# A hybrid decoder step on one core: the sample tile's expert queries with rows stationary, the projection's prelude, the norm turn and the w_out product

## The chip, the cores and the metric

One Trainium2 chip, one core. The metric is device time of one launch in microseconds (us), as the median over runs. Engines: PE is TensorE (PEld its weight load), ACT ScalarE, DVE VectorE, POOL GpSimd, SP SyncE. All data are fp32.

## The reference, cut to what matters

```python
h = x + merged @ w_out
n2 = rms_norm(h, ln2_g)
y = h + peer(n2)                                  # 1024 prompt rows and 8*4 = 32 sample rows

def blk(xb):                                      # PEER: 8 heads, 128 keys per half, 16 experts per head
    qh = (xb @ wq).reshape(128, 8, 2, 128)
    s = einsum('thcd,hckd->thck', qh, keys)
    sv, si = top_k(s, 16)
    ...                                           # 16x16 candidates, top 16 of them: eidx, gates gw
    hpre = einsum('td,thkd->thk', xb, u_tab[eidx])
    act = gelu(hpre) * gw
    return einsum('thk,thkd->td', act, v_tab[eidx])
```

Ahead of it one projection of all rows is made: `rms_norm(x, ln1_g) @ w_in` (1024 x 11280), and `rms_norm(mem, mem_norm_g) @ w_mem_kv` for 256 memory rows. Attention and gated linear attention between the two stages are not touched.

## The kernel before, in words

**Projection (`project`).** Eleven tiles are normed and transposed first: eight of 128 prompt rows, one of 32 sample rows, two of memory rows. For each, SP loads the rows into one of two buffers `xin` (L166), ACT makes the root (square L268, logarithm L271, exponential L274), DVE scales the rows into `xn` (L313), PE transposes them in two halves (L335), ACT copies each half as the high part (L215) and DVE takes the low part (L222). ACT takes the root of tile t+1 before it copies tile t, DVE likewise. Then the first chunk of w_in (470 columns of 24 chunks) is split into high and low parts (ACT L228, DVE L233), and a loop of 12 pairs of chunks begins: PE makes three partial products for each of eight tiles (L344), and for the sample tile products on four column groups (`quarters`, L350: 32 stationary columns, 118 moving). Memory products come last. POOL loads w_in, and its first two chunks are asked for at the start. ACT's queue also moves caches and joins the two expert tables into `scratch_uv`.

**Experts (`experts`).** A turn is one head of one prompt tile (64 turns), or four heads of the 32 sample rows together (turns 64 and 65). Each turn has 16 rows k. POOL gathers row k's 128 table rows (8 KB each, L2233) into one of eight slots; DVE makes the dot product (L2437); ACT makes gelu, weight and a diagonal matrix (L2284, L2288, L2296); PE adds diagonal times row to the sum, two products of 512 columns (`sum_row`, L2571), which frees the slot. The order on every engine is written out by hand: PE runs `sum_row(turn, k)` for k = 0 to 15 and between them the queries of turn+3 (L2540, behind k = 4), its scores (L2553, behind k = 7), and for the next tile the transposed rows. Once per tile the next tile's `h` is made: merged rows are transposed (L2492, turn 1 of the tile, k = 8), the w_out product's 16 parts run behind odd k of turns 2 and 3 (L2503), DVE adds and squares in turn 4, ACT takes the root behind `exponents` of k = 8 in turn 4 (L2279, L2253, L2255), DVE norms the rows. Gelu and exponential lie in different tables of ACT, so each change between them is a load. The load of merged rows for the next tile is issued by SP after the previous tile's outputs are stored, which happens behind k = 3 of turn 0.

## Time and profile before

| | us |
|---|---|
| median of 3 runs | 4892.18 (4890.57 to 4895.22) |
| profiled execution | 4897.54 |
| its span | 4895.9 |
| mean granted clock of TensorE | 0.954 of full |

The profile's page gives busy time by engine, the chain of waits followed back from the last instruction, and groups of instructions by line. The trace behind it can be asked for any stretch. In the page TensorE is busy 86% of the span, VectorE 51%, ScalarE 36%, GpSimd 30%; DMA moves 335 GB/s on average. The projection fills the first 1153 us, the experts' stage the last 2800 us.

### The profile page before, as it was taken

Reading aid. Unit: us, or ns where it says so; the run is one execution under the profiler, and the core shown is the slowest. Engines: PE = TensorE matmul, PEld = TensorE weight load, DVE = VectorE, ACT = ScalarE, POOL = GpSimd, SP = SyncE. Lnnn points to the kernel's source line nnn. Section 1 sums busy time; section 2 is a strip of 40 time slices with the busy share of each in tenths; the row PEclk is TensorE's granted clock in tenths of the full one; section 3 lists DMA queues with packets and bytes.
Section 4 is the critical chain, followed back from the end, with each engine's and each line's share of the span. In section 5 each row is a group of like instructions: output and inputs, shape, how many; then the busy total and the mean of one; then the engine's idle time right before and its main releaser. Section 6 shows DMA issues by size and latency. Waiting matters only on the chain.

```text
span 4895.9 us, 55849 instructions
## 1 busy us (share of the span) xinstructions
PE 4225.6 (86%) x18768; PEld 2548.2 (52%) x18768; DVE 2516.4 (51%) x5454; ACT 1774.2 (36%) x4676; POOL 1491.4 (30%) x1435
## 2 busy tenths in 40 slices
PE   6999999996556788979889889898898888988997
PEld 5888888885434565434334344344343443433361
DVE  3111111115741673546666666666666666666645
ACT  3110111113511464324444444444444444444433
POOL 0000000003720551124444434344344444444433
PEclk9999999997668899989999999999999999999989
DMA  7799897882367783679999999999999999999979
GB/s 268 251 324 320 292 320 277 298 284 94 101 216 270 235 244 119 247 285 421 420 420 402 421 416 407 421 416 411 421 404 420 416 412 421 410 411 417 403 298 384
DMA packets 317396, 1642.02 MB, mean 335 GB/s; under 512 B 43832, under 2 KB 85656, under 8 KB 175224
## 3 DMA queue, kind: packets, MB, share of 16 engines
q0 software_dynamic: 164720, 1168.36, 58.3%
q1 hardware_dynamic: 116464, 248.64, 14.9%
q10 hardware_dynamic: 35984, 222.30, 13.6%
q8 instruction: 104, 1.70, 0.1%
q14 instruction: 124, 1.02, 0.1%
HBM read 1550.39 MB, written 318.03 MB: 382 GB/s over the span
## 4 chain that ended last, share of the span: by engine, by line
DMA 31%; PE 17%; ACT 4%; issue 3%; POOL 1%; DVE 0%; DVEq 0%; POOLq 0%; SPq 0%; ACTq 0%; PEldq 0%
DMA ex_rows<-scratch_uv,ex_E 31%; PE ex_ps_y L2571 13%; PE ex_ps_q L2540 3%; PE ex_ps_t L2503 1%; ACT ex_diag L2296 1%; POOL ex_rows L2233 1%; ACT ex_w L2288 1%; ACT ex_gel L2284 1%; ACT L2284 0%; ACT L2279 0%; ACT L2255 0%; ACT L2253 0%; PE ex_ps_s L2553 0%; PE ex_ps_y L2565 0%; DVE ex_dots L2437 0%
## 5 line engine op out<-in xcount | busy, mean ns | idle before, releaser
L2571 PE MATMUL ex_ps_y<-ex_rows,ex_diag 128*128 128x512 f32 (+1 forms) x4224 | 2016.0, 612 | 322.4 <-ACT ex_diag L2296 302.2
L2437 DVE CUSTOM_DVE_ANT_0 ex_rows<-ex_rows,ex_n2u 128x1024 f32<-128x1024 f32 x1056 | 1294.6, 1226 | 945.8 <-DMA ex_rows<-scratch_uv,ex_E 937.4
L2233 POOL DMA_INDIRECT ex_rows<-scratch_uv,ex_E x1056 | 1136.3, 1076 | 1681.4 <-PE ex_ps_y L2571 1547.9
L2571 PEld LDWEIGHTS ex_ps_y<-ex_rows,ex_diag 128*128 128x128 f32 (+1 forms) x4224 | 746.3, 189 | 1484.2 <-ACT ex_diag L2296 762.0
L344 PE MATMUL pj_ps<-pj_w_hi,pj_nT 128*128 128x470 f32 x3072 | 699.1, 378 | 23.0 <-PE pj_ps L350 13.1
L2284 ACT ACTIVATE ex_gel<-ex_dots 128x1 f32<-128x1 f32 x1056 | 214.0, 203 | 1361.9 <-DVE ex_dots L2437 1360.8
L344 PEld LDWEIGHTS pj_ps<-pj_w_hi,pj_nT 128*128 128x128 f32 x3072 | 580.2, 189 | 108.2 <-issue 28.8
L248 DVE COPY pj_zo<-pj_ps 128x470 f32<-128x470 f32 x96 | 61.4, 646 | 718.7 <-PE pj_ps L344 536.1
L2296 ACT ACTIVATE ex_diag<-ex_ident,ex_w 128x128 f32<-128x128 f32 x1024 | 411.1, 401 | 34.0 <-PE ex_ps_y L2571 0.5
L344 PE MATMUL pj_ps<-pj_w_lo,pj_nT 128*128 128x470 f32 x1536 | 362.3, 378 | 0.0
L248 ACT COPY pj_zo<-pj_ps 128x470 f32<-128x470 f32 x96 | 52.0, 553 | 826.3 <-PE pj_ps L344 484.3
L197 POOL DMA_DIRECT2D pj_w<-in_w_in x22 | 19.4, 883 | 1007.6 <-PE pj_ps L350 878.4
L2288 ACT ACTIVATE ex_w<-ex_gel,ex_gates 128x1 f32<-128x1 f32 x1056 | 311.1, 295 | 38.6 <-ACT ex_gel L2284 0.4
L344 PEld LDWEIGHTS pj_ps<-pj_w_lo,pj_nT 128*128 128x128 f32 x1536 | 291.9, 190 | 38.6
L2540 PEld LDWEIGHTS ex_ps_q<-ex_n2T,ex_wq 128*128 128x128 f32 x2304 | 287.1, 204 | 31.6 <-issue 30.1
L2540 PE MATMUL ex_ps_q<-ex_n2T,ex_wq 128*128 128x128 f32 (+1 forms) x2304 | 287.6, 286 | 1.1 <-ACT ex_n2T L2262 1.1
L233 DVE TENSOR_TENSOR pj_w_lo<-pj_w,pj_w_hi 128x3760 fp32r<-128x3760 f32 x28 | 114.1, 4074 | 159.9 <-ACT pj_w_hi L228 159.9
L2503 PE MATMUL ex_ps_t<-wo,ex_mT 128*128 128x512 f32 (+1 forms) x288 | 147.4, 603 | 1.1 <-ACT ex_mT L2244 1.1
L1516 PE MATMUL at_ps_b<-wb,at_ogT 128*128 128x512 f32 (+1 forms) x288 | 139.0, 604 | 9.4 <-DMA wb<-in_w_br_gla 7.4
L2096 PE MATMUL mg_ps_b<-wb,mg_aT 128*128 128x512 f32 (+1 forms) x288 | 129.0, 606 | 1.1 <-ACT mg_aT L2008 1.1
L1279 POOL TENSOR_TENSOR at_xr<-at_x,at_stat 128x1024 f32<-128x1024 f32 (+1 forms) x34 | 55.9, 1644 | 183.9 <-ACT at_stat L1315 82.8
L228 ACT CAST pj_w_hi<-pj_w 128x3760 fp32r<-128x3760 f32 x28 | 93.7, 3346 | 34.5 <-DMA pj_w<-in_w_in 23.1
(368 smaller groups left out, 3667.4 us busy)
## 6 DMA issues: line engine op xcount, KB each, us to landing
pj_w<-in_w_in POOLq DMA_DIRECT2D x24, 1880.0 KB, 18.0
scratch_z<-pj_zo SPq DMA_DIRECT2D x192, 235.0 KB, 10.9
scratch_uv<-in_peer_u ACTq DMA_DIRECT2D x8, 4096.0 KB, 25.4
scratch_uv<-in_peer_v ACTq DMA_DIRECT2D x8, 4096.0 KB, 43.0
scratch_uv<-in_peer_u ACTq DMA_DIRECT2D x4, 8192.0 KB, 41.6
scratch_uv<-in_peer_v ACTq DMA_DIRECT2D x4, 8192.0 KB, 72.1
out_dk_s<-in_cache_dil_k ACTq DMA_DIRECT2D x8, 4088.0 KB, 43.3
out_dv_s<-in_cache_dil_v ACTq DMA_DIRECT2D x8, 4088.0 KB, 55.2
```

The source lines that it names most:

```text
L233: nc.vector.tensor_tensor(w_lo[:, slot], w[:, slot], w_hi[:, slot], ALU.subtract).then_inc(w_lo_done, 1)
L344: last = nc.tensor.matmul(out, rows(a, k), weights(b, k), start=(m == 0 and k == 0), stop=(m == 2 and k == KD - 1))
L1516: last = nc.tensor.matmul(ps_b[0:width(t)], ogT[:, k, 0:width(t)], wb[:, k, 512 * half:512 * half + 512], start=(k == 0), stop=(k == KD - 1))
L2096: last = nc.tensor.matmul(ps_b[0:n, i % BANKS], aT[:, j, k, 0:n], wb[:, KD + k, 512 * c:512 * c + 512], start=(k == k0), stop=(k == k1 - 1))
L2233: pool.indirect_dma_start(out=rows[:, p % SLOTS, :], out_offset=None, in_=d["uv"], in_offset=bass.IndirectOffsetOnAxis(ap=E[:, turn % 4, k ...
L2284: nc.scalar.activation(gel[:, j, k:k + 1], dots[:, j, k:k + 1], ACT.Gelu).then_inc(gel_done, 1)
L2288: nc.scalar.mul(w[:, j, k:k + 1], gel[:, j, k:k + 1], gates[:, turn % 4, k:k + 1]).then_inc(w_done, 1)
L2296: nc.scalar.mul(diag[:, p % DIAGS, :], ident[:], w[:, j, k:k + 1]).then_inc(diag_done, 1)
L2437: nc.vector.tensor_tensor_reduce(out=row, in0=row, in1=n2u[:, tile % 2], scale=1.0, scalar=0.0, op0=ALU.mult, op1=ALU.add, accum_out=dots[ ...
L2503: last = nc.tensor.matmul(ps_t[0:n, 4 * c:4 * c + 4].rearrange("p k t -> p (k t)"), mT[:, k, 0:n], wo[:, k, 512 * c:512 * c + 512], start= ...
L2540: last = nc.tensor.matmul(ps_q[:, at:at + n], wq[:, k, head * 256 + c * P:head * 256 + (c + 1) * P], n2T[:, k, 0:n], start=(k == 0), stop= ...
L2571: last = nc.tensor.matmul(y[0:n, 512 * c:512 * c + 512], diag[:, p % DIAGS, 0:n], rows[:, p % SLOTS, D + 512 * c:D + 512 * c + 512], start ...
```

## The change

In `experts`: the two sample turns' queries are no longer 64 products with the weights stationary (128 columns) and 32 rows moving, but 32 products with the 32 rows stationary and 256 columns of weights moving, four heads at four groups of 32 output partitions, in two halves; ACT copies them to `qT`, PE transposes them, ACT copies again. An ordinary turn's queries are cut in two halves, behind k = 2 and k = 4. The w_out product's parts are spread over turns 0 to 3, the merged rows are transposed in turn 0 behind k = 7 (copied behind k = 9). In the norm turn one table set is loaded before the exponentials.

In `project`: three buffers of rows, asked for ahead of the constants; the weight loads wait for the second tile's landing; the first chunk is split behind tile 5; the two memory tiles are left out of the prelude, their roots are taken behind loop pass 7 and their transposes run between passes 8 and 9 and 9 and 10, so that each loop is cut into several.

```diff
@@ project
-        sq = zo[:].rearrange("p b c -> p (b c)")[:, 0:D]
+        spare = zo[:].rearrange("p b c -> p (b c)")
+        sq = spare[:, 0:D]
+        x_at = [xin[:, 0], xin[:, 1], spare[:, D:2 * D]]
+        HELD, SPLIT_AT = XT, 5
+        EARLY = 9
...
+            load_x(0)
             sp.dma_start(g1[:], d["ln1_g"].partition_broadcast(P)).then_inc(consts_in, 16)
+            load_x(1)
+            sp.dma_start(ident[:], d["ident"]).then_inc(consts_in, 16)
+            load_x(2)
             sp.dma_start(gm[:], d["mem_norm_g"].partition_broadcast(P)).then_inc(consts_in, 16)
-            sp.dma_start(ident[:], d["ident"]).then_inc(consts_in, 16)
...
             pool.sem_inc(w_used, 2)
+            pool.wait_ge(x_in[1], 16)
             for c in range(2):
                 pool.dma_start(w[:, c], w_dram[:, :, c * CW:(c + 1) * CW]).then_inc(w_in[c], 16)
...
-            take_hi(act, len(tiles) - 1)
-            split_hi(act, 0, 0, 0)
+            root(0)
+            for t in range(1, HELD):
+                root(t)
+                take_hi(act, t - 1)
+                if t == SPLIT_AT:
+                    split_hi(act, 0, 0, 0)
+            take_hi(act, HELD - 1)
...
+            root(HELD)
+            root(HELD + 1)
+            last_joins(DEC_B, EARLY)
+            take_hi(act, HELD)
+            last_joins(EARLY, EARLY + 1)
+            take_hi(act, HELD + 1)
+            last_joins(EARLY + 1, CHUNKS // 2)
...
+            chunk_pairs(0, EARLY)
+            turned(HELD)
+            chunk_pairs(EARLY, EARLY + 1)
+            turned(HELD + 1)
+            chunk_pairs(EARLY + 1, CHUNKS // 2)
@@ experts
+    OUT_AT = [(0, 14)] + [(turn, k) for turn in (1, 2, 3) for k in (0, 8, 10, 12, 14)]
...
+            def packed_queries(turn):
+                act.wait_ge(qs_done, turn - NT * PH + 1)
+                act.wait_ge(s_done, turn)
+                nc.scalar.copy(qT[:], ps_q[:, 0:2 * P]).then_inc(qs_out, 1)
...
+                        if k == 4 and packs(turn + 3):
+                            packed_queries(turn + 3)
...
+                    norms = k == 8 and turn % PH == 4 and turn < NT * PH
+                    if norms:
+                        nc.scalar.preload_act_table_set(TABLES)
                     if k == 8 and turn + 2 < TURNS:
                         exponents(turn + 2)
...
+            def packed_queries(turn, ks):
+                if 0 in ks:
+                    if opens(turn):
+                        pe.wait_ge(n2T_out, NT + 1)
+                    pe.wait_ge(qT_out, turn)
+                for k in ks:
+                    for i, head in enumerate(heads_of(turn)):
+                        last = nc.tensor.matmul(ps_q[i * NS:(i + 1) * NS, 0:2 * P], n2T[:, k, 0:NS], wq[:, k, head * 256:(head + 1) * 256],
+                                                start=(k == 0), stop=(k == KD - 1), skip_group_check=True)
+                if KD - 1 in ks:
+                    last.then_inc(qs_done, 1)
+            def turn_queries(turn):
+                pe.wait_ge(qs_out, turn - NT * PH + 1)
+                for c in range(2):
+                    last = nc.tensor.transpose(ps_q[:, (2 + c) * P:(3 + c) * P], qT[:, c * P:(c + 1) * P], ident[:])
+                last.then_inc(q_done, 1)
...
-                        if k == 4:
-                            queries(turn + 3)
+                        if packs(turn + 3):
+                            if k in (2, 3):
+                                packed_queries(turn + 3, range(4 * (k - 2), 4 * (k - 1)))
+                            if k == 5:
+                                turn_queries(turn + 3)
+                        elif k in (2, 4):
+                            queries(turn + 3, (k // 2 - 1,))
...
-                        if k == 8 and turn % PH == 1:
+                        if k == 7 and turn % PH == 0:
                             turn_merged(tile_of(turn) + 1)
-                        if k % 2 == 1 and turn % PH in (2, 3):
-                            out_product(tile_of(turn) + 1, (turn % PH - 2) * KD + k // 2)
+                        if (turn % PH, k) in OUT_AT:
+                            out_product(tile_of(turn) + 1, OUT_AT.index((turn % PH, k)))
```

PE's order in the turn that prepares turn 64, from the transposed sample rows (`ex_n2u`) to the scores. `ex_ps_y` is a row sum (two products each), `ex_ps_q` the queries; "x" is how many stand in a row. Before:

```order
L2524 MATMUL ex_ps_t<-ex_ident,ex_n2u 128x32 x8
L2571 MATMUL ex_ps_y<-ex_rows,ex_diag 128x512 x6
L2540 MATMUL ex_ps_q<-ex_n2T,ex_wq 128x32 x64
L2571 MATMUL ex_ps_y<-ex_rows,ex_diag 128x512 x6
L2553 MATMUL ex_ps_s<-ex_keysT,ex_qT 32x128 x8
```

The same place in the changed kernel:

```order
L2601 MATMUL ex_ps_t<-ex_ident,ex_n2u 128x32 x8
L2667 MATMUL ex_ps_y<-ex_rows,ex_diag 128x512 x2
L2628 MATMUL ex_ps_q<-ex_wq,ex_n2T 32x256 x16
L2667 MATMUL ex_ps_y<-ex_rows,ex_diag 128x512 x2
L2628 MATMUL ex_ps_q<-ex_wq,ex_n2T 32x256 x16
L2667 MATMUL ex_ps_y<-ex_rows,ex_diag 128x512 x4
L2637 MATMUL ex_ps_q<-ex_ident,ex_qT 128x128 x2
L2667 MATMUL ex_ps_y<-ex_rows,ex_diag 128x512 x4
L2649 MATMUL ex_ps_s<-ex_keysT,ex_qT 32x128 x8
```

64 products in one block have become two blocks of 16, with a row's sum between them, and two transposes.

ACT's order in the norm turn, behind row 8: `ex_ex` are the exponentials of turn+2, `ex_stat` the root. Before:

```order
L2279 ACT_TABLE_LOAD
L2279 ACTIVATE ex_ex,ex_esum<-ex_ex 128x16
L2253 ACT_TABLE_LOAD
L2253 ACTIVATE ex_stat<-ex_stat,ex_eps 128x1
L2255 ACT_TABLE_LOAD
L2255 ACTIVATE ex_stat<-ex_stat 128x1
L2284 ACT_TABLE_LOAD
L2284 ACTIVATE ex_gel<-ex_dots 128x1
```

The same place in the changed kernel:

```order
L2411 ACT_TABLE_LOAD
L2352 ACTIVATE ex_ex,ex_esum<-ex_ex 128x16
L2320 ACTIVATE ex_stat<-ex_stat,ex_eps 128x1
L2322 ACTIVATE ex_stat<-ex_stat 128x1
L2357 ACT_TABLE_LOAD
L2357 ACTIVATE ex_gel<-ex_dots 128x1
```

The two middle loads are gone.

PE's order in turn 3 of a tile, from behind row k = 1 to behind k = 7; `ex_ps_t` is a part of the w_out product. Before:

```order
L2503 MATMUL ex_ps_t<-wo,ex_mT 128x512
L2571 MATMUL ex_ps_y<-ex_rows,ex_diag 128x512 x4
L2503 MATMUL ex_ps_t<-wo,ex_mT 128x512
L2571 MATMUL ex_ps_y<-ex_rows,ex_diag 128x512 x2
L2540 MATMUL ex_ps_q<-ex_n2T,ex_wq 128x128 x16
L2571 MATMUL ex_ps_y<-ex_rows,ex_diag 128x512 x2
L2503 MATMUL ex_ps_t<-wo,ex_mT 128x512
L2571 MATMUL ex_ps_y<-ex_rows,ex_diag 128x512 x4
L2553 MATMUL ex_ps_s<-ex_keysT,ex_qT 128x128 x2
L2503 MATMUL ex_ps_t<-wo,ex_mT 128x512
```

Turns 1 to 3 in the changed kernel, from behind row k = 0 to behind k = 8:

```order
L2580 MATMUL ex_ps_t<-wo,ex_mT 128x512
L2667 MATMUL ex_ps_y<-ex_rows,ex_diag 128x512 x4
L2615 MATMUL ex_ps_q<-ex_n2T,ex_wq 128x128 x8
L2667 MATMUL ex_ps_y<-ex_rows,ex_diag 128x512 x4
L2615 MATMUL ex_ps_q<-ex_n2T,ex_wq 128x128 x8
L2667 MATMUL ex_ps_y<-ex_rows,ex_diag 128x512 x6
L2649 MATMUL ex_ps_s<-ex_keysT,ex_qT 128x128 x2
L2667 MATMUL ex_ps_y<-ex_rows,ex_diag 128x512 x2
L2580 MATMUL ex_ps_t<-wo,ex_mT 128x512
```

In rows 0 to 7 of turns 2 and 3 stood four parts and one query block of 16; now there is one part, in turns 1 to 3, and the block is in two.

## Rows read from the trace of the kernel before

**Rows 1.** The page, part 4: the chain that ended last, shares of the span.
```profile
DMA ex_rows<-scratch_uv,ex_E 31%; PE ex_ps_y L2571 13%; PE ex_ps_q L2540 3%; PE ex_ps_t L2503 1%; ACT ex_diag L2296 1%; POOL ex_rows L2233 1%; ACT ex_w L2288 1%; ACT ex_gel L2284 1%; ACT L2284 0%; ACT L2279 0%; ACT L2255 0%; ACT L2253 0%; P
```

**Rows 2.** Stretches: length, busy us of engines (instructions), TensorE clock, DMA share, GB/s.
```profile
2500.00:4636.00 2136.00, 1887.35 (x5556) 867.04 (x5555) 1423.12 (x3567) 960.35 (x2854) 897.79 (x833) 0.99 1.01 414
2672.00:2696.00 24.00, 21.77 (x52) 9.64 (x52) 16.77 (x42) 11.67 (x36) 13.07 (x10) 0.93 0.93 366
2696.00:2896.00 200.00, 169.38 (x502) 75.96 (x501) 130.60 (x329) 89.14 (x266) 77.65 (x78) 1.00 1.01 421
4536.00:4636.00 100.00, 98.72 (x292) 42.13 (x293) 68.27 (x173) 41.93 (x131) 45.64 (x39) 1.00 1.00 405
4640.00:4664.00 24.00, 19.07 (x45) 7.97 (x45) 15.15 (x37) 11.31 (x34) 10.18 (x10) 0.86 1.00 383
4672.00:4712.00 40.00, 40.00 (x168) 30.13 (x168) 15.11 (x33) 11.29 (x35) 7.84 (x9) 0.70 0.53 208
4728.00:4768.00 40.00, 40.00 (x174) 29.44 (x174) 15.77 (x34) 11.98 (x36) 8.36 (x10) 0.74 0.66 262
```

**Rows 3.** The chain in turn 18 (third tile): start, us, engine, tile, line.
```profile
2905.50 3.57 PE ex_ps_q L2540 x32
...
2910.79 0.86 PE ex_ps_t L2503 x2
2911.65 3.43 PE ex_ps_y L2571 x8
2915.08 0.44 PE ex_ps_s L2553 x4
```

**Rows 4.** The chain: the sample tile's two query blocks.
```profile
4670.82 23.66 PE ex_ps_q L2540 x128
...
4727.13 22.09 PE ex_ps_q L2540 x128
```

**Rows 5.** Timeline of TensorE, projection: start, us, shape, count [idle before].
```profile
104.73 1.82 PE L350 MATMUL pj_ps<-pj_w,pj_nS 128*32 128x118 f32 x64
...
106.97 1.97 PE L344 MATMUL pj_ps<-pj_w_hi,pj_nT 128*128 128x470 f32 x8 [0.42 <-PE pj_ps L350]
```

**Rows 6.** Timeline of ScalarE, norm turn of the third tile, first and last of four loads.
```profile
2995.59 1.28 ACT L2279 ACT_TABLE_LOAD   x1
...
3000.33 1.28 ACT L2284 ACT_TABLE_LOAD   x1
```

**Rows 7.** Timeline of TensorE: behind the norm turn's loads, and in an ordinary turn.
```profile
3002.64 18.77 PE L2571 MATMUL ex_ps_y<-ex_rows,ex_diag 128*128 128x512 f32 x36 [5.04 <-ACT ex_diag L2296]
...
3080.00 2.41 PE L2571 MATMUL ex_ps_y<-ex_rows,ex_diag 128*128 128x512 f32 x5 [0.96 <-ACT ex_diag L2296]
```

**Rows 8.** Timeline of the projection's start, all engines.
```profile
2.67 31.04 SPq L166 DMA_DIRECT2D pj_xin<-in_x_prompt  x8
...
16.49 1.05 ACT L215 CAST pj_nT<-pj_ps 128x512 fp32r<-128x512 f32 x2
...
26.09 0.59 ACT L215 CAST pj_nT<-pj_ps 128x512 fp32r<-128x512 f32 x1 [0.62 <-PE pj_ps L335]
...
39.20 0.59 ACT L215 CAST pj_nT<-pj_ps 128x512 fp32r<-128x512 f32 x1 [0.62 <-PE pj_ps L335]
...
46.32 0.48 DVE L222 TENSOR_TENSOR pj_nT<-pj_ps,pj_nT 128x128 fp32r<-128x128 f32 x2
...
46.75 1.94 PE L335 MATMUL pj_ps<-pj_ident,pj_xn 128*128 128x128 f32 x8 [1.32 <-DVE pj_nT L222]
...
53.13 3.33 ACT L228 CAST pj_w_hi<-pj_w 128x3760 fp32r<-128x3760 f32 x1
...
56.49 4.07 DVE L233 TENSOR_TENSOR pj_w_lo<-pj_w,pj_w_hi 128x3760 fp32r<-128x3760 f32 x1 [2.53 <-ACT pj_w_hi L228]
...
60.70 3.50 PE L344 MATMUL pj_ps<-pj_w_hi,pj_nT 128*128 128x470 f32 x8 [8.09 <-DVE pj_w_lo L233]
```

**Rows 9.** The experts' loads of merged rows: from issue to landing.
```profile
DMA to landing us min/median/max: 9.1/11.6/20.6
```

More of the change, by code:

```diff
@@ L307, in _, with normed @@
             dve.wait_ge(consts_in, 48)
-            for t, (row, n, mem) in enumerate(tiles):
+            def normed(t):
+                row, n, mem = tiles[t]
                 dve.wait_ge(rms_done, t + 1)
@@ L328, in _, with turned @@
             pe.wait_ge(consts_in, 48)
-            for t, (row, n, mem) in enumerate(tiles):
+            def turned(t):
+                row, n, mem = tiles[t]
                 pe.wait_ge(xn_done, t + 1)
@@ L338, in _ @@
                     last.then_inc(halves_done, 1)
-            pe.wait_ge(lo_out, 2 * len(tiles))
+            for t in range(HELD):
+                turned(t)
+            pe.wait_ge(lo_out, 2 * HELD)
             def product(out, rows, weights):
@@ L2178, in heads_of, with packs @@
             return [turn % PH] if turn < NT * PH else [(turn - NT * PH) * PACK + i for i in range(PACK)]
+        def packs(turn):
+            return turn >= NT * PH
         def width(tile):
@@ L2267, in queries @@
                     act.wait_ge(s_done, turn)
[L2268 removed]
+                nc.scalar.copy(qT[:], ps_q[:, 2 * P:] if packs(turn) else ps_q[:, 0:2 * P]).then_inc(qT_out, 1)
+            def packed_queries(turn):
+                act.wait_ge(qs_done, turn - NT * PH + 1)
+                act.wait_ge(s_done, turn)
+                nc.scalar.copy(qT[:], ps_q[:, 0:2 * P]).then_inc(qs_out, 1)
             def scores(turn):
@@ L2525, in turn_rows, with queries @@
                 last.then_inc(n2_t, 1)
-            def queries(turn):
-                tile, heads = tile_of(turn), heads_of(turn)
-                n = width(tile)
-                if opens(turn):
-                    pe.wait_ge(n2T_out, tile + 1)
-                if turn == 1:
-                    pe.wait_ge(wq_in, 16)
-                if turn:
-                    pe.wait_ge(qT_out, turn)
-                for i, head in enumerate(heads):
-                    for c in range(2):
-                        at = (2 * i + c) * n
-                        for k in range(KD):
-                            last = nc.tensor.matmul(ps_q[:, at:at + n], wq[:, k, head * 256 + c * P:head * 256 + (c + 1) * P], n2T[:, k, 0:n],
-                                                    start=(k == 0), stop=(k == KD - 1))
+            def queries(turn, halves=(0, 1)):
+                tile, (head,) = tile_of(turn), heads_of(turn)
+                if 0 in halves:
+                    if opens(turn):
+                        pe.wait_ge(n2T_out, tile + 1)
+                    if turn == 1:
+                        pe.wait_ge(wq_in, 16)
+                    if turn:
+                        pe.wait_ge(qT_out, turn)
+                for c in halves:
+                    for k in range(KD):
+                        last = nc.tensor.matmul(ps_q[:, c * P:(c + 1) * P], wq[:, k, head * 256 + c * P:head * 256 + (c + 1) * P], n2T[:, k],
+                                                start=(k == 0), stop=(k == KD - 1))
+                if 1 in halves:
+                    last.then_inc(q_done, 1)
```

105 lines of the change are left out of this document (63 added, 42 removed).

## The prediction

> **What bounds the kernel now.** Read the chain of waits first [rows 1]. It reaches back only to the start of the experts' stage (2096 us, the last 2800 us of the span), and two thirds of it there is gathers landing and the row sums behind them. So the first question is how full the DMA engines are, and the table of stretches answers it [rows 2]. In a quiet stretch (2696 to 2896) the engines move 421 GB/s, share 1.01: nothing but fewer bytes would help there. A gather is 128 rows of 8 KB, 1.05 MB, so 2.49 us at that rate, and a turn of 16 gathers cannot take under 39.8 us. Time is lost only where the rate falls below 421. I turn each rate into lost time as length x (421 - rate)/421, and ask which edit removes that loss.
>
> The losses fall in three places [rows 2]. (a) The two turns that prepare the sample tile's queries: 4672 to 4712 at 208 GB/s loses 20.2 us, 4728 to 4768 at 262 loses 15.1 us; 35.3 us together. (b) A 24 us stretch after the norm turn of each tile, at 366 in 2672 and 383 in 4640: 3.1 and 2.2 us. (c) The 100 us before it, in which the w_out product is interleaved; in the last tile they run at 405, 3.8 us lost. The row 2500 to 4636 holds the rest of (b) and (c): 414 over 2136 us loses 35.5 us for six norm turns and seven product stretches, and the norm turn at 4640 adds 2.2, so 37.7 us. I give (b) 7 x 2.9 = 20 us and the rest, 17 us, to (c), 2.4 us per tile.
>
> Why a stall of TensorE becomes lost DMA time: a gather needs one of eight row slots, and a slot is free only when TensorE has summed its row. TensorE needs 1.72 us per row (3.43 us for two) against 2.49 us per gather [rows 3], so it catches up 0.77 us per row, 12 us per turn.
>
> The stage before, the projection, is a different case: there TensorE issues products back to back from 60.70 us on, so whatever delays the first product delays everything [rows 8].
>
> **The change, part by part.**
>
> *Packed queries.* Before, each of the two turns issues 64 products of 32 columns against a full 128x128 weight load: 23.66 and 22.09 us during which no row is summed [rows 4]. TensorE's clock there reads 0.70 and 0.74 of full as a mean, so much of it runs at 1.2 GHz instead of 2.4 [rows 2]. Afterwards there are 32 products of 256 columns, the rows stationary (32 columns), four heads on four column groups, in two halves behind rows 2 and 3, then a copy and two transposes behind row 5. The trace has this very shape: the projection's sample quarters, 32 products of 118 columns on four groups, took 1.82 us [rows 5]. Scaled by 256/118 that is 3.9 us per turn. Streamed without any overlap between groups, at half of the 512-column product's 0.86 us [rows 3], it would be 32 x 0.43 = 13.7 us. I take 3.9, since only the row of the quarters has the four groups. That is the size of an ordinary turn's query block, 3.57 us [rows 3], which costs no DMA time in the quiet stretch, and it now comes in halves of 2 us. The additions: two transposes of about 0.24 us each (8 took 1.94 us) [rows 8], a second copy, and TensorE's wait for that copy behind row 5. ScalarE makes it after diagonal 4, before TensorE gets to row 5, so two row sums (3.4 us) hide it; behind ScalarE's own wait for the products stands the weight of row 5, due a gather later. I charge 1.3 us for both turns. **Gain 34 us**, ends 24 (no overlap: 27.4 us of products instead of 45.8, the excess over the catch-up lost) and 35.3.
>
> Around the quarters TensorE is idle for 0.42 us before the next full-width product [rows 5]; eight such edges in the two turns come to 3.4 us spread over 80 us, below the catch-up. The Trainium skill ("TensorEngine Tiling (Array Packing)", Key Properties) says that changing the tiling mode drains TensorE, which speaks against splitting the queries into halves; the trace agrees that there is a gap, and puts 0.42 us on it. The term stays 34 us by either.
>
> *Norm turn.* ScalarE loads four tables in a row, 1.28 us each, from 2995.59 to 3001.61 [rows 6]; TensorE waits 5.04 us and then needs 18.77 us for nine rows, 2.09 each instead of 1.72, at a lower clock [rows 2, 7]. An ordinary turn has two loads and a wait of 0.96 us [rows 7], and its stretch shows no loss. With the set that holds both logarithm and exponential loaded ahead, the two middle loads go: 2 x 1.28 = 2.57 us off ScalarE in each of eight tiles, and what remains is an ordinary turn plus 0.5 us. Tile 0's norm turn lost almost nothing, so seven count. **Gain 18 us** of 20; ends 8 (only the 2.57 us of ScalarE count, and TensorE arrives late from (c) anyway) and 20.
>
> The Trainium skill ("ScalarE: Activation LUTs", What ACT_TABLE_LOAD costs) gives a switch about 2.66 us, half of it a drain ahead of the load. Here four loads of 1.28 us and the activations between them fill 6.02 us in all, with no room for drains, so the measurement decides; by the page the edit would take 5.3 us off each norm turn instead of 2.57, which could not return more than the 20 us lost.
>
> *w_out and the split of ordinary queries.* Eight products of 0.86 us per turn behind odd rows of turns 2 and 3 become one in turn 0 and five in each of turns 1 to 3; the query block of 3.57 us is cut in two, behind rows 2 and 4. TensorE's load in turns 2 and 3 was 16 x 1.72 + 3.57 + 0.44 + 8 x 0.86 = 38.4 of 39.8 us; now 35.8 in turns 1 to 3. Between rows 0 and 7 it was 7.4 us of extras against 8 x 0.77 = 6.2 of catch-up; now 4.9. That turns a deficit into a surplus. **Gain 11 us** of 17; ends 2 (the total of products is the same, and turn 1 now has them as well) and 17. The merged rows are transposed behind row 7 of turn 0 rather than row 8 of turn 1. They are requested right after the previous tile's outputs (row 3) and land 11.6 us later [rows 9]; four rows at 2.49 us plus 1.5 MB of other traffic at 421 (3.6 us) make 13.5 us, so the wait is about nothing. Queued behind it on TensorE would be the row sums.
>
> *Prelude.* The first product waits for the whole chain of eleven tiles, then for the first weight chunk's split, 3.33 on ScalarE and 4.07 on VectorE [rows 8]. The sample tile's low parts were done at 46.80. Now (1) the tiles' rows are asked for first and the weights after the second tile has landed. From the first tile's copy at 16.49 to the third's at 26.09 pass 9.6 us, where two steady steps are 6.6 (26.09 to 39.20 are four steps, 3.28 each): 3.0 us, and the first request moves up from 2.67 to the place of the first constant, 1.8 us, together 4.8; (2) the split sits in the chain after tile 5 and adds 3.33 on ScalarE and about 2.4 where VectorE's 4.07 holds up the next norm. First product at 46.8 - 4.8 + 5.7 = 47.7 instead of 60.70: 13.0 us. Against it, the two memory tiles are transposed on TensorE inside the projection, 2 x 1.94 us in full, and the loop is cut in three. No row shows such a cut; from one product group to the next TensorE idles 0.42 us [rows 5], so I add 1 us and keep 3 for the low end. Their roots and norms lie beside products on the other engines. **Gain 8 us**, ends 4 and 11.
>
> **Sum.** 34 + 18 + 11 + 8 = 71 us. The profiled execution spans 4895.9 us, 4897.54 with what lies around it, 5.4 above the median of 4892.18. Losses of 71 us from it and from the median are the same work, so I predict 4892 - 71 = **4821 us**. All terms at their low ends give 38 (4854), all at their high ends 83 (4809).
>
> **Rivals.**
> *No overlap of the column groups*: halves of 6.9 us; the term falls to 24, so 4831. For: matmuls of one shape run in order. Against: the quarters' 1.82 us. 8 in 100.
> *The norm and w_out losses move instead of going*: rates stay near 365 and 412 because the slots, not the bursts, limit them, and turn 1 joins in. Gain 34 + 8 + 8, so 4842. For: the amount of products is unchanged. Against: the quiet stretches at 421 with the same slots. 13 in 100.
> *The prelude gives nothing*: the tables' and caches' transfers now start when the products do, and the first banks wait for their stores: 4829. 7 in 100.
> *Slower*: the merged rows come late. If their load took 20.6 us, the longest one [rows 9], rather than 11.6, TensorE would stand 9 us behind row 7 in each of eight tiles, 72 us, plus the 3 us of low clock that the norm turn's 5 us wait shows, 24 us: 71 - 96 = 25 us slower, 4917. It decides from about 5.5 us of extra landing time per tile. Against: seven loads of this place have the median 11.6, the longest is from the stage's start. 2 in 100.
> Main case 70 in 100.
>
> **Chances.** A measurement of this kernel can tell about 0.2% (10 us) from no change. All cases but the last are faster by more: 0.96, within 0.02, slower 0.02. The range of 8 in 10 runs from 4806 (all high ends and 3 us more) to 4846 (the second rival with a smaller prelude).
>
> **What would show it.** Right: query groups of the sample turns with 64 entries of 32x256 taking about 4 us, no stretch near 4700 below 400 GB/s; two table loads in a norm turn, its stretch near 420; 100 us before it near 418; first product near 48 us and no gap of TensorE at loops above 2 us. Wrong: products of 0.4 us one after another; a wait of TensorE for the h rows in turn 0; the lost rate found again at rows 8 to 15 of turns 0 and 1.

## The result

| | us | |
|---|---|---|
| before | 4893.1 | 4890.57 to 4895.22, 4 runs |
| changed | **4851.53** | 4850.49 to 4852.78, 4 runs |
| ratio | 0.9909 | 95% interval 0.9897 to 0.9922 |
| forecast | 4821 | range 4806 to 4846 |

The change is faster by 41.6 us, where 71 were forecast. The direction was right; the size was wrong, and the time lies 5.5 us outside the range. The profiled execution took 4852.27 us with a span of 4850.6, against 4895.9 before.

Put beside [rows 2], the table of stretches after (columns as there: length, busy us of PE, PEld, DVE, ACT and POOL with their instructions, TensorE's granted clock, DMA share, GB/s). In order: the quiet part of the stage, the second tile's norm turn with its two loads, 200 us of an ordinary stretch, the last tile's product stretch, its norm turn, and the two turns with the packed queries.

```profile
2500.00:4620.00 2120.00, 1893.40 (x5534) 870.65 (x5533) 1418.52 (x3555) 933.41 (x2828) 971.76 (x830) 0.99 1.01 416
2656.00:2680.00 24.00, 19.28 (x44) 7.24 (x42) 16.67 (x38) 12.06 (x37) 11.78 (x10) 1.00 1.01 411
2696.00:2896.00 200.00, 174.58 (x501) 79.64 (x501) 130.18 (x330) 87.56 (x263) 90.02 (x78) 0.98 1.01 418
4520.00:4620.00 100.00, 94.92 (x283) 41.57 (x284) 69.88 (x179) 41.95 (x131) 46.94 (x40) 1.00 1.00 413
4624.00:4648.00 24.00, 17.23 (x34) 6.83 (x35) 15.07 (x34) 8.92 (x29) 12.40 (x9) 0.93 1.01 392
4656.00:4696.00 40.00, 35.14 (x158) 13.72 (x154) 27.09 (x72) 17.93 (x55) 18.34 (x17) 1.00 1.01 415
4700.00:4740.00 40.00, 32.65 (x84) 11.58 (x83) 26.91 (x68) 17.98 (x55) 18.20 (x17) 1.00 1.01 421
```

The packed turns are as forecast: 415 and 421 GB/s instead of 208 and 262, at the full clock of 2.4 GHz. The norm turns rose only part of the way to the 420 of the forecast: 411 instead of 366 GB/s in the second tile, 392 instead of 383 in the last. The product stretch has 413 instead of 405, where 418 was forecast. And the row over the whole quiet part says 416 instead of 414, where the two terms for it (18 and 11 us) asked for 419.

TensorE in the first packed turn, timeline (start, us, line, shape, count, idle before in brackets):

```profile
4654.53 1.02 PE L2667 MATMUL ex_ps_y<-ex_rows,ex_diag 128*128 128x512 f32 x2
4655.48 1.93 PE L2628 MATMUL ex_ps_q<-ex_wq,ex_n2T 128*32 128x256 f32 x32
4657.35 3.70 PE L2667 MATMUL ex_ps_y<-ex_rows,ex_diag 128*128 128x512 f32 x8
4660.88 0.38 PE L2637 MATMUL ex_ps_q<-ex_ident,ex_qT 128*128 128x128 f32 x2
4661.10 3.60 PE L2667 MATMUL ex_ps_y<-ex_rows,ex_diag 128*128 128x512 f32 x8
```

A half takes 1.93 us (1.95 were forecast from [rows 5]), the transposes 0.38, and TensorE waits for nothing between. The gap of 0.42 us at a change of shape [rows 5], which the Trainium skill's "TensorEngine Tiling (Array Packing)" (Key Properties) leads one to fear for eight edges, does not stand here: between full-width row sums and column groups no idle time is listed. (In the projection such a gap is still there: 0.55 us at 843.10 below.)

ScalarE's loads and TensorE's wait in the second tile's norm turn, against [rows 6, 7]:

```profile
2657.98 1.28 ACT L2411 ACT_TABLE_LOAD   x1
...
2660.02 1.28 ACT L2357 ACT_TABLE_LOAD   x1
...
2662.33 5.42 PE L2667 MATMUL ex_ps_y<-ex_rows,ex_diag 128*128 128x512 f32 x12 [2.33 <-ACT ex_diag L2369]
```

The same turn of the kernel before:

```profile
2673.74 17.41 PE L2571 MATMUL ex_ps_y<-ex_rows,ex_diag 128*128 128x512 f32 x36 [4.08 <-ACT ex_diag L2296]
```

Two loads instead of four, and a wait of 2.33 us instead of 4.08. The projection, against [rows 8]:

```profile
47.35 3.10 PE L397 MATMUL pj_ps<-pj_w_hi,pj_nT 128*128 128x470 f32 x7 [1.14 <-DVE pj_nT L234]
...
843.10 1.07 PE L385 MATMUL pj_ps<-pj_ident,pj_xn 128*128 128x128 f32 x8 [0.55 <-PE pj_ps L403]
```

The first product starts at 47.35 (47.7 forecast, 60.70 before), and a memory tile's eight transposes inside the loop take 1.07 us, not 1.94.

So the loads, the waits and the products came out as forecast, the rates rose at least part of the way, and 30 us are missing. The page's chain has the gathers at 36% of the span (31% before, [rows 1]) and the row sums at 9% (13%): the stage was bound by landings before and is bound by them now.

```profile
DMA ex_rows<-scratch_uv,ex_E 36%; PE ex_ps_y L2667 9%; PE ex_ps_q L2615 1%; ACT ex_diag L2369 1%; ACT ex_w L2361 1%; PE ex_ps_t L2580 1%; ACT ex_gel L2357 1%; ACT L2357 0%; ACT L2352 0%; PE ex_ps_y L2661 0%; DVE ex_dots L2514 0%; DVE ex_rows L2514 0%; POOL ex_rows L2300 0%; ACT ex_mT L2311 0%; ACT ex_ex L2352 0%
```

### The profile page after: what moved, and what is told of

Read it like the earlier page. It is cut to its first block, busy times and chain, and to the rows that moved or that the text cites. A ratio compares the mean times of both kernels' runs of the same rounds, so it can differ in the third digit from the quotient of the medians.

```text
span 4850.6 us, 55532 instructions
## 1 busy us (share of the span) xinstructions
PE 4210.5 (87%) x18644; PEld 2516.7 (52%) x18644; DVE 2514.9 (52%) x5454; ACT 1748.6 (36%) x4662; POOL 1586.1 (33%) x1435
## 4 chain that ended last, share of the span: by engine, by line
DMA 36%; PE 12%; issue 4%; ACT 4%; DVE 1%; POOL 0%; DVEq 0%; POOLq 0%; ACTq 0%; SPq 0%; PEldq 0%
DMA ex_rows<-scratch_uv,ex_E 36%; PE ex_ps_y L2667 9%; PE ex_ps_q L2615 1%; ACT ex_diag L2369 1%; ACT ex_w L2361 1%; PE ex_ps_t L2580 1%; ACT ex_gel L2357 1%; ACT L2357 0%; ACT L2352 0%; PE ex_ps_y L2661 0%; DVE ex_dots L2514 0%; DVE ex_rows L2514 0%; POOL ex_rows L2300 0%; ACT ex_mT L2311 0%; ACT ex_ex L2352 0%
## 5 line engine op out<-in xcount | busy, mean ns | idle before, releaser
L2300 POOL DMA_INDIRECT ex_rows<-scratch_uv,ex_E x1056 | 1231.8, 1167 | 1548.0 <-PE ex_ps_y L2667 1401.8
L2615 PEld LDWEIGHTS ex_ps_q<-ex_n2T,ex_wq 128*128 128x128 f32 x2048 | 250.6, 193 | 59.9 <-issue 56.7
L2615 PE MATMUL ex_ps_q<-ex_n2T,ex_wq 128*128 128x128 f32 x2048 | 251.5, 277 | 1.1 <-ACT ex_n2T L2329 1.1
```

The costliest lines, as they stand in the source:

```text
L2300: pool.indirect_dma_start(out=rows[:, p % SLOTS, :], out_offset=None, in_=d["uv"], in_offset=bass.IndirectOffsetOnAxis(ap=E[:, turn % 4, k ...
L2615: last = nc.tensor.matmul(ps_q[:, c * P:(c + 1) * P], wq[:, k, head * 256 + c * P:head * 256 + (c + 1) * P], n2T[:, k], start=(k == 0), st ...
```

## Where the missing time was: nowhere

The forecast turned each rate below 421 GB/s into lost time. The trace of the kernel before had the means to test that. VectorE makes a row's dot product the moment the row has landed, so its starts are the landings. Here they are through the third tile's norm turn, the very place at which ScalarE loads four tables (2995.59 to 3001.61), TensorE waits 5.04 us [rows 6, 7] and the rate dips to 373 GB/s; rows in between are left out:

```profile
2996.00:3020.00 24.00, 18.96 (x38) 7.91 (x37) 17.32 (x40) 14.16 (x38) 10.92 (x9) 0.86 0.93 373
```

```profile
2998.31 1.23 DVE L2437 CUSTOM_DVE_ANT_0 ex_rows<-ex_rows,ex_n2u 128x1024 f32<-128x1024 f32 x1 [1.16 <-DMA ex_rows<-scratch_uv,ex_E]
...
3000.79 1.22 DVE L2437 CUSTOM_DVE_ANT_0 ex_rows<-ex_rows,ex_n2u 128x1024 f32<-128x1024 f32 x1 [0.64 <-DMA ex_rows<-scratch_uv,ex_E]
...
3005.76 1.23 DVE L2437 CUSTOM_DVE_ANT_0 ex_rows<-ex_rows,ex_n2u 128x1024 f32<-128x1024 f32 x1 [0.19 <-DMA ex_rows<-scratch_uv,ex_E]
...
3008.24 1.23 DVE L2437 CUSTOM_DVE_ANT_0 ex_rows<-ex_rows,ex_n2u 128x1024 f32<-128x1024 f32 x1 [1.16 <-DMA ex_rows<-scratch_uv,ex_E]
...
3023.15 1.23 DVE L2437 CUSTOM_DVE_ANT_0 ex_rows<-ex_rows,ex_n2u 128x1024 f32<-128x1024 f32 x1 [0.40 <-DMA ex_rows<-scratch_uv,ex_E]
```

From 2998.31 to 3023.15 stand ten steps in 24.84 us: 2.484 each, the full pace, through the stall. (Between 3000.79 and 3005.76 one dot product started late, behind VectorE's own norm; the next stands at its place again.) In the second tile's norm turn, the one of [rows 2] with 366 GB/s, a single landing is 0.32 us late. Nothing was lost there, so nothing could be won.

That gives a theory. **Theory A:** landings go on at 2.485 us as long as a stall of TensorE is shorter than what the eight row slots hold in flight; only what goes beyond is lost. **Rival B:** the forecast's reading, each us of a lower rate is lost. Both explain the packed turns (stalls of 22 to 24 us); they part on everything short.

To compare kernels better than by medians, which differ by some us from chip to chip for the same kernel, I use two lengths of each trace: from the start of the second tile's first gather to that of the last prompt tile's (768 gathers), and from there to the end. The start of a gather is its issue, and a stall just ahead of it can move that without moving a landing; where this matters I count from the landing instead, that is from VectorE's first dot product of the second tile.

| kernel | six tiles | to the end | sum |
|---|---|---|---|
| before | 1969.7 | 462.7 | 2432.5 |
| changed | 1965.0 | 431.3 | 2396.3 |
| changed, another chip | 1967.2 | 431.2 | 2398.5 |

The two traces of the changed kernel differ by 2.2 us, and the spread is wider than that: the kernel before with the new prelude alone (below), whose experts' stage is unchanged, has a sum of 2427.7, 4.8 us less than the kernel before. The six tiles gave 3 to 5 us, which is within this spread; the last tile and the sample turns gave 31.4.

## Experiment 1: each part alone

**Packed queries alone**, in the kernel before:

```diff
-                        if k == 4:
+                        if packs(turn + 3):
+                            if k in (2, 3):
+                                packed_queries(turn + 3, range(4 * (k - 2), 4 * (k - 1)))
+                            if k == 5:
+                                turn_queries(turn + 3)
+                        elif k == 4:
                             queries(turn + 3)
```

> The kernel before with the sample tile's packed queries alone. Theory A (gathers land at the DMA's own pace, 2.49 us each, and only a stall longer than the row slots cover delays a landing): the landings of turns 61 and 62 were late by 14.6 and 13.0 us plus some 3.7 us around them in the trace of before; 29 to 32 us faster. Rival B (every microsecond at a rate below 421 GB/s is lost time): 34 to 35 us faster.

Measured: 4865.96 us (4864.88 to 4869.3), ratio 0.9942 [0.9928, 0.9955], 28.4 us less than before. That is below the range of either theory, and the interval (22 to 35 us) holds both. The sum of the table is 2397.8, which is 34.6 us below the kernel before and 29.9 below the unchanged stage of the next run. So this run cannot tell A from B. It shows where the gain is: with 2396.3 and 2398.5 for the changed kernel, the whole of its gain behind the projection is in this part.

**Prelude alone** (`project` of the changed kernel, the rest of the kernel before):

```diff
+            load_x(0)
             sp.dma_start(g1[:], d["ln1_g"].partition_broadcast(P)).then_inc(consts_in, 16)
+            load_x(1)
...
+            chunk_pairs(0, EARLY)
+            turned(HELD)
+            chunk_pairs(EARLY, EARLY + 1)
+            turned(HELD + 1)
```

> The kernel before with the projection's new prelude alone. The projection ended 10.5 us earlier in the changed kernel's trace, but the experts began only 7.5 us earlier. Theory A and B alike: 8 to 10.5 us faster if the stages between are neutral; 5 to 7.5 if the 3 us lost between them belong to the change.

Measured: 4880.37 us (4878.78 to 4882.47), ratio 0.9971 [0.996, 0.9981], 14.0 us less, more than either expected. The projection's last product ended at 1138.7 instead of 1152.9, 14.2 us earlier. The products' loop gives back next to nothing of the 13.4 us by which the first product moved up: the sample tile's product groups start 13.7 us earlier in the first pass and in the last (91.0 against 104.7, 1101.2 against 1114.9), since the two passes that carry transposes are 0.6 us longer and the others about 0.1 us shorter. Between the projection and the experts stands a stage that no edit touches. It takes 990.6 to 998.2 us from trace to trace, so what the prelude is worth is read from the projection and from the medians, not from where one trace's experts begin. In the changed kernel's own first trace the last product ended at 1142.3: one pass lost 2.8 us there, in which TensorE waits 2.09 us for VectorE's split of a weight chunk, and its second trace (1139.1) has nothing of it.

**Table load ahead of the norm turn's exponentials, alone:**

```diff
+                    norms = k == 8 and turn % PH == 4 and turn < NT * PH
+                    if norms:
+                        nc.scalar.preload_act_table_set(TABLES)
                     if k == 8 and turn + 2 < TURNS:
                         exponents(turn + 2)
```

> The kernel before with one table set loaded ahead in the norm turn (16 of 32 loads fewer over eight tiles). Theory A: the dots went on at 2.49 us through the stall, so 0 to 3 us faster. Rival B: the dips to 366 GB/s are lost time, 16 to 20 us faster.

Measured: 4899.93 us (4891.98 to 4904.48, 11 runs), ratio 1.001 [1.0001, 1.0019], so 5.6 us more, with an interval that just excludes zero; sum of the table 2432.7 against 2432.5. A had 0 to 3 us less. The traces show no change in the stage, and what makes the median higher is open. There is no gain where the forecast had 18 us. B falls.

**The w_out product spread, merged rows earlier, ordinary queries in halves, alone:**

```diff
-                        if k == 8 and turn % PH == 1:
+                        if k == 7 and turn % PH == 0:
                             turn_merged(tile_of(turn) + 1)
-                        if k % 2 == 1 and turn % PH in (2, 3):
-                            out_product(tile_of(turn) + 1, (turn % PH - 2) * KD + k // 2)
+                        if (turn % PH, k) in OUT_AT:
+                            out_product(tile_of(turn) + 1, OUT_AT.index((turn % PH, k)))
```

> The kernel before with the w_out product spread over turns 0 to 3, merged rows transposed in turn 0 and ordinary queries in halves; nothing else. Theory A: landings of turns 2 and 3 were late by 0.5 to 1 us per tile, so 2 to 6 us faster. Rival B: 11 to 17 us faster.

Measured: 4891.95 us (4887.59 to 4898.06, 11 runs), ratio 0.9993 [0.9984, 1.0002], 2.4 us less. Its sum in the table is 2423.9, which is 8.6 us less than before but only 3.8 less than the unchanged stage in the prelude's run; one trace of each, so I leave it at somewhere between 0 and 9 us.

**Packed queries and prelude together, without the other two:** the same question from the other side.

> The kernel before with the packed sample queries and the new prelude alone, without the table load ahead of the norm turn's exponentials and without the spread of the w_out product, the earlier merged rows and the halves of ordinary queries. Theory A (landings go on through stalls shorter than the slots' cover): those parts are worth 0 to 5 us, so 4851 to 4857. Rival B (my forecast's reading, 18 and 11 us for them): 4875 to 4885.

Measured: 4848.15 us (4846.49 to 4851.82), ratio 0.9908 [0.9891, 0.9924]; sum of the table 2397.6. Against the kernel before on the same chip it is 45.4 us less, more than A's 36 to 42 and far from B. That is the changed kernel (ratio 0.9909 [0.9897, 0.9922], sums 2396.3 and 2398.5). Once the packed queries are in, the norm turn's edit and the w_out edit cannot be seen at all.

## Experiment 2: how long a stall the slots cover

A direct test of A: put stalls of known length where there were none. Into the changed kernel, with n = 1, 3 or 5:

```diff
+                    if k == 12 and turn % PH >= 5 and turn < NT * PH - 3:
+                        for i in range(n):
+                            nc.scalar.activation(stall[:, 2 * i:2 * i + 1], eps[:], ACT.Exp).then_inc(stalled, 1)
+                            nc.scalar.activation(stall[:, 2 * i + 1:2 * i + 2], eps[:], ACT.Gelu).then_inc(stalled, 1)
```

Each exponential and each gelu needs its own table set, so each pair costs ScalarE two loads, 3.03 us in all (loads of two neighbouring pairs start 3.03 us apart in the trace).

> The changed kernel with one pair of table loads more (a small exponential and a small gelu on a scratch column) on ScalarE behind row 12 of turns 5, 6 and 7 of each of the first seven tiles: 21 places, about 3.0 us each (two loads of 1.28 us and two small activations). TensorE then waits some 2.5 us for a diagonal. Theory A (a stall costs only what is beyond the cover of the eight row slots, 7 to 8 us): within 3 us of the changed kernel, 4849 to 4855. Rival B (every us of a lower rate is lost, my forecast's reading, by which a wait of 5 us costs 2.9): 1.5 us each, 31 more, 4875 to 4895.

> The same with three pairs in a row, about 9.0 us on ScalarE at the 21 places; TensorE waits about 8.5 us. Theory A: 0 to 1.5 us beyond the cover at each place, so 0 to 32 more, best guess 4870. Rival B: at least 5 us each, 105 more or over, 4955 to 4990.

> The same with five pairs in a row, about 15 us on ScalarE; TensorE waits about 14.5 us. Theory A: 14.5 less 7 to 8 of cover is 7 us each, 150 more (130 to 175), 4980 to 5025; from three pairs to five the whole 6 us of each place is paid, 126 us. Rival B: 8.7 us or more each, at least 183 more, 5035 or over, and it rises in proportion from one pair to five.

| pairs | TensorE waits | median (range) | ratio to before | sum of the table | from the second tile's first landing to the end |
|---|---|---|---|---|---|
| 0 | | 4851.53 | 0.9909 [0.9897, 0.9922] | 2396.3 | 2381.4 (2383.5 on another chip) |
| 1 | 1.1 to 1.9 us | 4847.89 (4845.0 to 4848.48) | 0.9899 [0.9883, 0.9916] | 2396.3 | 2381.4 |
| 3 | 6.6 to 8.0 us | 4853.31 (4852.39 to 4853.87) | 0.9912 [0.9896, 0.9929] | 2396.3 | 2385.4 |
| 5 | 12.5 to 14.0 us | 4979.12 (4976.4 to 4986.28) | 1.0174 [1.0157, 1.0191] | 2508.8 | 2498.4 |

The cost has a knee. Three pairs cost next to nothing: 2 to 4 us of landings for the 18 stalls behind the second tile's first landing, and a median 5.4 us above that of one pair on the same chip, for 21 stalls; at most 0.3 us each, for waits of 7.4 us on average. (The sum of the table hides this, since a stall of the first tile delays the issue at which it begins by 4 us.) From three pairs to five the median rises 125.8 us for 21 stalls, 6.0 each, and ScalarE's two pairs more are 6.06 us: from there on every us is paid. Against one pair, five cost 6.2 us each of a mean wait of 13.2, so some 7 us are covered. A's range held for three pairs, though its best guess of 4870 was too high, and it missed for five by 0.9 us (4980 to 5025), since the waits were 1.3 us shorter than expected. B's straight line (at least 105 us for three pairs) is gone.

Three pairs, TensorE's wait, then VectorE's starts and the rate of the 24 us around it:

```profile
3410.34 9.86 PE L2676 MATMUL ex_ps_y<-ex_rows,ex_diag 128*128 128x512 f32 x18 [7.09 <-ACT ex_diag L2371]
```

```profile
3403.10 1.22 DVE L2523 CUSTOM_DVE_ANT_0 ex_rows<-ex_rows,ex_n2u 128x1024 f32<-128x1024 f32 x1 [1.17 <-DMA ex_rows<-scratch_uv,ex_E]
3405.59 1.22 DVE L2523 CUSTOM_DVE_ANT_0 ex_rows<-ex_rows,ex_n2u 128x1024 f32<-128x1024 f32 x1 [1.18 <-DMA ex_rows<-scratch_uv,ex_E]
3408.39 1.22 DVE L2523 CUSTOM_DVE_ANT_0 ex_rows<-ex_rows,ex_n2u 128x1024 f32<-128x1024 f32 x1 [1.42 <-DMA ex_rows<-scratch_uv,ex_E]
3410.83 1.22 DVE L2523 CUSTOM_DVE_ANT_0 ex_rows<-ex_rows,ex_n2u 128x1024 f32<-128x1024 f32 x1 [0.81 <-DMA ex_rows<-scratch_uv,ex_E]
```

```profile
3396.00:3420.00 24.00, 16.91 (x35) 7.14 (x34) 16.61 (x44) 17.05 (x42) 10.13 (x9) 0.86 1.00 406
```

The same for five pairs:

```profile
3429.31 12.21 PE L2676 MATMUL ex_ps_y<-ex_rows,ex_diag 128*128 128x512 f32 x24 [13.17 <-ACT ex_diag L2371]
```

```profile
3430.89 1.23 DVE L2523 CUSTOM_DVE_ANT_0 ex_rows<-ex_rows,ex_n2u 128x1024 f32<-128x1024 f32 x1 [0.38 <-DMA ex_rows<-scratch_uv,ex_E]
3438.64 1.23 DVE L2523 CUSTOM_DVE_ANT_0 ex_rows<-ex_rows,ex_n2u 128x1024 f32<-128x1024 f32 x1 [6.09 <-DMA ex_rows<-scratch_uv,ex_E]
3442.09 1.23 DVE L2523 CUSTOM_DVE_ANT_0 ex_rows<-ex_rows,ex_n2u 128x1024 f32<-128x1024 f32 x1 [1.43 <-DMA ex_rows<-scratch_uv,ex_E]
```

```profile
3416.00:3440.00 24.00, 10.83 (x22) 4.74 (x22) 13.35 (x39) 18.57 (x43) 5.46 (x5) 0.72 0.69 278
```

Three pairs: a wait of 7.09 us, and the landings come 2.49, 2.80 and 2.44 us apart. TensorE's row sums of 1.7 us against 2.49 us per landing let it catch up behind the stall before the next one. Five pairs: 13.17 us, and the step from 3430.89 to 3438.64 is 7.75 us, 5.3 late, the next one 3.45, another 1.0 late. The slots ran dry, as A has it; that it is the eight slots which set the 7 us is argued, for no run has another number of them. The DMA share comes nearer to telling them apart than the rate: 1.00 with three pairs, 0.69 with five, and 0.53 and 0.66 in the two sample query blocks of the kernel before, but 1.00 in the norm turn at 4640 and the product stretch at 4536 [rows 2], from which the forecast took its 2.2 and 3.8 us of loss. It is no measure either: at 2672 it was 0.93, with 0.32 us of delay.

## Experiment 3: what the rest of a tile's time is

128 gathers at 2.485 us are 318.1 us, a tile takes 327.5. In every tile landings are late at two kinds of places. Four gathers in turn 0 (k = 6 to 9) are 0.2 to 1.3 us late, together about 4 us, where outputs are stored and the next h and x rows come in. The others stand alone: a landing 0.97 us late every 21 to 25 gathers, five or six per tile, at the same rows in kernels whose TensorE, ScalarE or GpSimd work differs. With the projection of the kernel before, in which VectorE's program is another, the same pattern stands at other rows. In the changed kernel I count 39 of them in tiles two to eight. One of them in VectorE's timeline, 3.45 us behind its neighbour where the others are 2.48 apart:

```profile
3231.20 1.23 DVE L2514 CUSTOM_DVE_ANT_0 ex_rows<-ex_rows,ex_n2u 128x1024 f32<-128x1024 f32 x1 [1.09 <-DMA ex_rows<-scratch_uv,ex_E]
...
3233.68 1.23 DVE L2514 CUSTOM_DVE_ANT_0 ex_rows<-ex_rows,ex_n2u 128x1024 f32<-128x1024 f32 x1 [1.16 <-DMA ex_rows<-scratch_uv,ex_E]
...
3237.13 1.28 DVE L2514 CUSTOM_DVE_ANT_0 ex_rows<-ex_rows,ex_n2u 128x1024 f32<-128x1024 f32 x1 [1.60 <-DMA ex_rows<-scratch_uv,ex_E]
```

So regular an interval, counted in rows and not in time, suggests the loading of some engine's program. Three kernels lengthen one program each, by four semaphore increments per row that nobody waits for:

```diff
+                    for _ in range(4):
+                        pool.sem_inc(filler, 1)
```

(behind each gather on GpSimd; the same with `pe` behind each row's sum on TensorE, and with `dve` behind each dot product on VectorE.)

> The changed kernel with four more semaphore increments per gather in GpSimd's queue, which do nothing but lengthen its program. If the late landings of 0.97 us that come about every 58 us (every 23.5 gathers) come with the fetching of GpSimd's program, they come about every 14 gathers instead: some 32 more of them, 25 to 40 us slower, and the rate in the experts' stage falls to about 412 GB/s. If not: within 4 us of the changed kernel. The reading of rates as lost time has no view on this.

> The changed kernel with four more semaphore increments per row in TensorE's queue, which do nothing but lengthen its program, by about a third per row. If the late landings of 0.97 us come with the fetching of TensorE's program, they come about every 17 or 18 gathers instead of every 23.5: about 15 more in the stage, 12 to 18 us slower than the changed kernel, 4862 to 4869, and they stand at other rows than before. If not: within 4 us of it, and the late landings at the same rows.

> The changed kernel with four more semaphore increments per row in VectorE's queue. If the late landings come with the fetching of VectorE's program (some 8 instructions a row, so half as many again): about 22 more of them, 18 to 24 us slower, 4868 to 4875. If not: within 4 us of the changed kernel, and the late landings at the same rows.

And one that shortens VectorE's, with the changed kernel once more beside it:

```diff
-                if p >= 2 * K:
-                    dve.wait_ge(gel_done, p - 2 * K + 1)
+                if p >= 2 * K and k == 0:
+                    dve.wait_ge(gel_done, p - K)
```

> The changed kernel, with VectorE's wait for the gelu of two turns ago made once per turn (for all 16 of that turn) instead of ahead of each dot product: 15 waits fewer per turn, nothing else. From the intervals of 23.5 gathers between late landings with the changed kernel and 13.5 with four instructions more per row, a transfer of VectorE's program holds about 127 instructions and a row takes 5.4 of them; with 0.94 fewer the interval is 28.4 gathers, 37 late landings in the stage instead of 45, 7 to 8 us faster than the changed kernel, 4841 to 4845. If the waits took no instructions of their own, or the late landings came for another reason: no difference, and the same rows late.

> The changed kernel itself once more, to stand beside the run with fewer waits on the same chip: 4846 to 4852, late landings every 23.5 gathers.

The queues that load instructions, from the page of each kernel (packets, MB, share): changed, GpSimd longer, TensorE longer, VectorE longer, VectorE shorter.

```profile
q8 instruction: 111, 1.82, 0.2%
q14 instruction: 124, 1.02, 0.1%
```

```profile
q14 instruction: 157, 1.29, 0.1%
```

```profile
q8 instruction: 128, 2.10, 0.2%
q14 instruction: 125, 1.02, 0.1%
```

```profile
q8 instruction: 111, 1.82, 0.2%
q14 instruction: 157, 1.29, 0.1%
```

```profile
q14 instruction: 117, 0.96, 0.1%
```

| kernel | packets more | gathers between late landings | sum of the table | median (range) | ratio to before |
|---|---|---|---|---|---|
| changed | | 21 to 25 | 2396.3, 2398.5 | 4851.53; 4845.57 (4842.81 to 4849.6) | 0.9909; 0.9898 [0.9882, 0.9915] |
| GpSimd longer | 33 | 21 to 25, same rows | 2395.8 | 4850.48 (4846.98 to 4852.22) | 0.9908 [0.9891, 0.9924] |
| TensorE longer | 17 | 21 to 25, same rows | 2396.4 | 4845.49 (4844.41 to 4850.77) | 0.9904 [0.9888, 0.9921] |
| VectorE longer | 33 | 12 to 15 | 2430.0 | 4882.9 (4876.72 to 4888.88) | 0.9975 [0.9965, 0.9984] |
| VectorE shorter | -7 | 23 to 32 | 2390.1 | 4841.85 (4837.27 to 4844.11) | 0.989 [0.9874, 0.9907] |

Only VectorE's program moves the late landings, in both directions. 33 packets more of its own cost 33.7 and 31.5 us against the two traces of the changed kernel, 1.0 us each; 7 fewer give back 6.2 and 8.4. (By medians the longer program costs 37.4 us against the kernel with TensorE's longer one on the same chip.) The arithmetic closes: four increments for each of 1056 rows are 4224 instructions, and 4224/33 is 128 per packet. The intervals say the same: if a packet holds N instructions and a row takes n, then N/n is 23 and N/(n+4) is 13.4, so n = 5.6 and N = 128; with 15/16 of an instruction fewer per row the interval should be 27.6, and it is 28 in the middle. The trace's records of single DMA packets agree. In the changed kernel 35 of 36 single late landings that I matched have a packet of 8 KB on q14 in the 6 us before them, with the longer program 65 of 66, nearly all of them 1.4 to 2.3 us before; of the 47 packets of q8 in the same stretch 6 and 8 have a late landing behind them.

My forecast for the longer program was 18 to 24 us; the interval came out as computed here, and the cost per late landing as well, so the size was off only because I had reckoned with eight instructions a row.

GpSimd's 33 packets more lie on the same queue and cost nothing. Why its packets and TensorE's don't delay a gather and VectorE's do is open.

The shorter program is the fastest kernel of the study. Beside the changed kernel on the same chip its median is 3.7 us lower, with ranges that overlap by 1.3 us; the traces, 6 to 8 us apart, and the moved rows make me take the gain as real, though the medians alone don't prove it.

## The forecast, step by step

- **Bound and catch-up.** (By [rows 1] gathers and row sums are 44% of the span, 2140 of the stage's 2800 us: three quarters, not two thirds. Nothing hangs on it.) That landings at 2.49 us set the stage was right, and so was the price of a row sum. What failed is the sentence "Time is lost only where the rate falls below 421. I turn each rate into lost time". A dip means that fewer bytes move in that stretch. With several gathers in flight, it does not mean that a gather lands late. Late landings are the loss, and they have to be counted themselves.
- **Packed queries, 34 us.** Mechanism and shape as forecast (1.93 us a half, 0.38 for the transposes, no wait). Measured 28.4 us by the median of the part alone. In the traces the last tile's landings went from 361.7 to 329.8 us, 32 us. Of the 35.3 us read from rates, the landings of the kernel before show 30.9: one 14.62 us late and its two followers 1.12 and 0.57, one 12.99 and 1.57. The rest was within the cover. The part that paid was the one in which the stalls (23.66 and 22.09 us, [rows 4]) exceeded it.
- **Norm turn, 18 us.** Nothing gained: 5.6 us slower by the medians of the part alone, no change in the traces. Its wait of 4 to 5 us is inside the 7 us that are covered. The edit does what it says (two loads instead of four, 411 GB/s instead of 366), to no gain. The low end of 8 us should have been 0: the range left out that a stall may cost nothing, although the text itself had the reason (TensorE catches up 12 us per turn, an ordinary wait is hidden).
- **w_out, 11 us.** Measured 2.4 alone, with an interval that holds zero, and nothing on top of the packed queries. Same step, same error: the deficit of 7.4 us of extras against 6.2 of catch-up is 1.2 us, far below the cover. The merged rows were not late, as forecast.
- **Prelude, 8 us.** Measured 14.0. The first product came at 47.35 instead of 47.7 forecast. Mis-sized was the charge against it: 2 x 1.94 us for the transposes and 1 us for the cuts, from rows of the prelude, in which each transpose waits for its copies. In the loop eight take 1.07 us and lengthen a pass by 0.6, and the cuts cost nothing visible: 1 us instead of 4.9. That is 3.9 of the 6.0 us; slightly shorter passes and an end of the loop 0.5 us quicker make 1.5 more in the trace.
- **Sum.** Parts alone: 28.4 - 5.6 + 2.4 + 14.0 = 39.2 us, the whole 41.6. The whole is 29.4 us short of 71: the norm and w_out terms measured -3.2 instead of 29 (32.2 less), packed queries 5.6 less, the prelude 6.0 more, and the whole is 2.4 more than its parts, which is within their intervals.
- **Rivals.** Nearest came "The norm and w_out losses move instead of going" (4842), with 13 in 100. Its time was closer than the main case's, but its mechanism is not what happened: the losses did not move, they were never there, or at most a few us of them. No overlap of the column groups, nothing from the prelude and late merged rows are all out. The two terms that gave nothing shared one assumption, so they fell together; the range, built as if they could fail apart, ended 5.5 us short.

## To carry over

Where transfers feed a ring of buffers, measure the landings (the consumer's starts), not the rate, and not the issues either: a stall upstream of the ring costs only what exceeds the buffers' cover, here some 7 us of TensorE's time with eight slots, and edits that shorten stalls below it are worth nothing. If several terms of a forecast rest on one reading of the profile, test that reading in the trace first, and let them fail together in the range. When a stream that only DMA bounds still shows evenly spaced late landings, count them in instructions of each engine: a shorter program of the right one pays.

## What the runs showed of the hardware

- Loading VectorE's program delays gathers: 0.97 us per packet of 8 KB, which holds 128 instructions by the counts and the intervals above; the 39 in tiles two to eight make 38 us of this kernel. Four semaphore increments per row, for which VectorE has time enough, cost 32 to 34 us in this way. The same on GpSimd or TensorE cost nothing. The Trainium skill ("Runtime: NRT & Kernel Launch", Instruction fetch mechanics) has programs refilled in blocks of 16 KiB, 256 instructions, at a cost that is mostly hidden. That agrees with TensorE's 16 KB packets here (4224 instructions in 17 of them, 248 each) and not with VectorE's: its packets have 8 KB, and in a stage bound by DMA each shows.
- Table loads on ScalarE are harmless while the ring covers them: 54 pairs in the six tiles (three at each of 18 places), about 164 us of ScalarE's time, moved the end by 2 to 4 us.
- Eight 128x128 transposes cost 1.07 us in a stream of products and 1.94 us in the prelude; 32-row column groups between full-width products showed no gap in the experts' stage, and 0.42 and 0.55 us in the projection.
- The granted clock fell to 0.86 in the stretch with three pairs and 0.72 with five, and to 0.94 and 0.93 as a mean of the whole run; with three pairs that cost next to nothing either.
